# Scaling two finished super-blocks by the last norm on POOL instead of DVE, in an fp32 streaming-encoder kernel

## The chip, the cores and the metric

One core of one Trainium2 chip runs the whole kernel. The metric is the device time in microseconds, the median of several runs.

## What is computed

One layer of a hybrid trunk over 2080 columns (2064 prompt frames with 16 learned ones in front, less the 16, plus 32 sampled ones), model width 1024, feed-forward width 2816, all in float32. A mixer (convolution, gated recurrence, pooled branch) gives x1; then comes the feed-forward part and a last RMS norm, which alone matters here:

```
x = x + (silu(g) * u) @ w_down          # [g | u] = RMSNorm(x) @ w_gu
y = x * rsqrt(mean(x*x, axis=-1) + 1e-6) * final_g
```

## The kernel before

All data lie transposed: the model width on 128 partitions times 8 tiles, frames along the free axis. The mixer runs over five blocks of 416 columns. Then the feed-forward part runs over three **super-blocks** `s` = 0, 1, 2 of 696, 692 and 692 columns (two halves of 348 or 346), and this part is the place of the change.

**Order of a super-block.** `STEPS` is gu0, gu1, gu2, dn0, gu3, gu4, dn1 and so on: gate/up passes over eleven pairs of feed-forward tiles, and down passes over five groups of them. A gate/up pass makes seven products (one level of Strassen's scheme), each from one weight slot of 128x1024. Every fp32 product is made of three matmuls on a high and a low part, so each slot is split first: SP loads it into `wraw`, ACT writes the high part (L878), DVE the low part (L1720), and TensorE waits for the low part (L684). The slots go round a ring of three, and a slot is refilled as soon as TensorE has left it. TensorE's matmuls are all at L704.

**DVE's other work** in a pass, in program order: it adds products from PSUM (L1625), multiplies gate and up (L1672), forms differences (L1674, L1676), writes low parts of the result (L1678, L1691, L1696, L1698), and reads the seventh product (L1682, L1685). In a down pass it adds products into `xacc` (L1711), the fp32 accumulator of the super-block, 8 tiles of 128 x 692 or 696.

**The last norm of super-block s** is spread over the first passes of super-block s+1. In pass 0 ACT squares and DVE sums; TensorE sums over partitions; in pass 1 ACT takes the root (L1122) and DVE the reciprocal (L1612), which leaves `nrstd`, one 128 x 696 tile. Then `finish` (L1617) scales the tiles of `xacc` in the order `NORM_ORDER`, one DVE operation a tile, at the places that `FINISH` names: four in pass 1, four at the start of pass 2. Each adds one to the semaphore `y_done`.

**Who waits for y_done.** POOL, whose loop (L670 to L679) stores each tile to the output as it is done (L678), then waits for the first four stores to have landed, loads four tiles of the next super-block's x1 into the same `xacc` (L604), waits for the last four stores and loads the other four. The first additions of down pass 0 (L1711) wait for these loads. And ACT, which in pass 2 waits for all eight (L1172) before it writes `hcomb` (L1174), since that part of `hcomb` lies over `nrstd`; ACT's later splits are queued behind this wait. After the last super-block DVE makes its eight `finish` operations with nothing beside them.

Of the kernel before, what the change touches and what calls it, by code (L numbers as in the profile page):

```python
# [8 lines left out]
KT = D // P  # L9
SEQ, META, DEC = 2048, 16, 32  # L10
NB = 5
# [22 lines left out]
TH = (348, 346, 346)  # L34
# [17 lines left out]
G1, CW0, CB, BR, BI, LAM, PSC, G2, GF = 0, 1, 5, 6, 7, 8, 9, 10, 11  # L52
# [124 lines left out]
RAWS = {(s, i): n for n, (s, _, i) in enumerate(STORED)}  # L177
NSIDE = 4 * NB + 4
NORM_ORDER = (0, 4, 1, 5, 2, 6, 3, 7)
FINISH = {(1, 1): (0,), (1, 2): (1,), (1, 3): (2,), (1, 4): (3,), (2, 0): (4, 5), (2, 1): (6, 7)}  # L180
CORDER = (0, 5, 1, 4, 2, 3, 6)
CFROM = {0: 11, 5: 11, 1: 11, 4: 11, 2: 3, 3: 7, 6: 11}
DIFFS = ("T1", "T3", "T2", "T4")
# [89 lines left out]
def build(nc, dx, dwm, dws, dcst, dfix, dst0, graw, draw, dy, dst, fused, sgu, sdn, x1s, ys):  # L273
# [4 lines left out]
    MUL, ADD, SUB = ALU.mult, ALU.add, ALU.subtract  # L278
    base = -(-nc.sbuf_base // 64) * 64
    ctx = ExitStack()  # L280
    with ctx:
        def sem(name):
            return ctx.enter_context(nc.semaphore(name))

        def at(offset, name, shape, dt=f32):
            return nc.alloc_sbuf_tensor_at(name, shape, dt, offset=base + offset)
# [5 lines left out]
        cst = at(37376, "cst", [P, NCST, KT])  # L292
# [27 lines left out]
        xacc = at(m0, "xacc", [P, KT, 2 * HW])  # L320
        hcomb = at(m0 + 22272, "hcomb", [P, 3, 2, 7, HW], f32r)
        nsq, ntot = at(m0 + 61248, "nsq", [P, 2, 2 * HW]), at(m0 + 66816, "ntot", [P, 2 * HW])
        nrstd, nsum = at(m0 + 69600, "nrstd", [P, 2 * HW]), at(m0 + 72384, "nsum", [P, 2, 2 * HW], f32r)
# [10 lines left out]
        n_sq, n_sum, n_hi, n_lo, n_rstd = sem("n_sq"), sem("n_sum"), sem("n_hi"), sem("n_lo"), sem("n_rstd")  # L334
# [22 lines left out]
            "xb_t", "xb_hist", "xb_saved", "wsum", "wfix", "d_done", "d_hi", "d_lo"))  # L357
        merged, m_hi, m_lo = sem("merged"), sem("m_hi"), sem("m_lo")
        h_hi, h_lo = sem("h_hi"), sem("h_lo")
        y_done = sem("y_done")  # L360
        block = ctx.enter_context(nc.Block())

        def bank(name):
# [167 lines left out]
        def _(pool):  # L531
# [68 lines left out]
            def load_acc(s):  # L600
                for n, m in enumerate(NORM_ORDER):
                    if s and n % 4 == 0:
                        pool.wait_ge(y_stored[n // 4], 16 * 4 * s)
                    pool.dma_start(xacc[:, m, 0:2 * TH[s]], x1s[m, :, TO[s]:TO[s] + 2 * TH[s]]).then_inc(x1_in[n // 4], 16)  # L604

            def quarter(s, kh, h, first, landed):

                cols = slice(TO[s] + h * TH[s], TO[s] + h * TH[s] + TH[s])
                pool.dma_start(work[:, first:first + 4, 0:TH[s]],
                               ys[4 * kh:4 * kh + 4, :, cols].rearrange("k p c -> p k c")).then_inc(landed, 16)  # L610

            def plain_quarters(s):
                if s:
                    pool.wait_ge(a_lo, 7 * s)
                quarter(s, 0, 0, 11, y_in[0])
                pool.wait_ge(a_lo, 7 * s + 1)
                quarter(s, 1, 0, 11, y_in[0])
                pool.wait_ge(a_lo, 7 * s + 2)
                quarter(s, 1, 1, 11, y_in[0])

            def mixed_quarters(s):
                quarter(s, 0, 0, 3, y_in[1])
                quarter(s, 0, 1, 7, y_in[2])

            def last_quarter(s):
                pool.wait_ge(a_lo, 7 * s + 6)
                quarter(s, 1, 0, 7, y_in[2])
# [42 lines left out]
            for s in range(NT - 1):  # L670
                pool.wait_ge(y_kept, 16 * KT * NB)
                plain_quarters(s + 1)
                pool.wait_ge(h_lo, 4 * PAIRS * (s + 1))
                mixed_quarters(s + 1)
                last_quarter(s + 1)
                for n, m in enumerate(NORM_ORDER):
                    pool.wait_ge(y_done, 8 * s + n + 1)
                    pool.dma_start(dy[m, :, TO[s]:TO[s] + 2 * TH[s]], xacc[:, m, 0:2 * TH[s]]).then_inc(y_stored[n // 4], 16)  # L678
                load_acc(s + 1)  # L679
# [648 lines left out]
        def _(dve):  # L1328
# [5 lines left out]
            def square_sum(kind, b, m):  # L1334
                n = sq_index(kind, b, m)
                width = W if (kind, b) == ("n1", 0) else LW
                dve.wait_ge(sq_done, n + 1)
                if m == 0:
                    V.tensor_copy(tot[:, 0:width], sq[:, n % 2, 0:width]).then_inc(sq_summed, 1)
                else:  # L1340
                    dve.wait_ge(sq_summed, n)
                    V.tensor_tensor(tot[:, 0:width], tot[:, 0:width], sq[:, n % 2, 0:width], ADD).then_inc(sq_summed, 1)

            def sum_rest(kind, b):
                dve.wait_ge(sum_hi, sum_index(kind, b) + 1)
                V.tensor_tensor(sums[:, 1, :], tot[:, 0:LW], sums[:, 0, :].bitcast(f32), SUB).then_inc(sum_lo, 1)

            def invert(name, q):
                b = name[1]
                width = LW if q else W  # L1350
                dve.wait_ge(*(clear(name) if name == ("n2", NB - 1, 0) else drain(name)))
                V.reciprocal(rstd[q][:, 0:width], rstd[q][:, 0:width]).then_inc(rstd_done[q], 1)
                dve.wait_ge(rstd_done[q], b if q == 1 else b + 1)
# [26 lines left out]
            def make_y(b, m):  # L1380
                if m == 0:
                    dve.wait_ge(x1_kept, 16 * KT * (b + 1))
                V.scalar_tensor_tensor(main[:, m, :], main[:, m, :], cst[:, G2, m:m + 1], rstd[2][:, 0:LW], MUL, MUL).then_inc(y_made, 1)
# [182 lines left out]
            def operand_lo(s, c):  # L1566
                w, q = TH[s], CORDER.index(c)
                dve.wait_ge(a_hi, 7 * s + q + 1)
                V.tensor_tensor(ycomb[:, c, 1, :, 0:w], work[:, CFROM[c]:CFROM[c] + 4, 0:w],
                                ycomb[:, c, 0, :, 0:w].bitcast(f32), SUB).then_inc(a_lo, 1)  # L1570
# [24 lines left out]
            def norm_sum(s, i):  # L1595
                n, w = KT * s + i, 2 * TH[s]
                dve.wait_ge(n_sq, n + 1)
                if i == 0:
                    V.tensor_copy(ntot[:, 0:w], nsq[:, n % 2, 0:w]).then_inc(n_sum, 1)
                else:  # L1600
                    dve.wait_ge(n_sum, n)
                    V.tensor_tensor(ntot[:, 0:w], ntot[:, 0:w], nsq[:, n % 2, 0:w], ADD).then_inc(n_sum, 1)

            def norm_rest(s):
                w = 2 * TH[s]
                dve.wait_ge(n_hi, s + 1)
                V.tensor_tensor(nsum[:, 1, 0:w], ntot[:, 0:w], nsum[:, 0, 0:w].bitcast(f32), SUB).then_inc(n_lo, 1)

            def norm_invert(s):
                w = 2 * TH[s]  # L1610
                dve.wait_ge(*clear(("n3", s, 0)))
                V.reciprocal(nrstd[:, 0:w], nrstd[:, 0:w]).then_inc(n_rstd, 1)  # L1612

            def finish(s, i):
                w, m = 2 * TH[s], NORM_ORDER[i]
                dve.wait_ge(n_rstd, s + 1)
                V.scalar_tensor_tensor(xacc[:, m, 0:w], xacc[:, m, 0:w], cst[:, GF, m:m + 1], nrstd[:, 0:w], MUL, MUL).then_inc(y_done, 1)  # L1617
# [9 lines left out]
            def beside(s, p, k):  # L1627


                if (p, k) == (0, 0):  # L1630
                    operand_lo(s, 6)
                if p == 0 and k < 4:
                    for i in (2 * k, 2 * k + 1):
                        if s:
                            norm_sum(s - 1, i)
                        else:
                            square_sum("n2", NB - 1, i)
                elif (p, k) == (0, 4):
                    if s:
                        norm_rest(s - 1)  # L1640
                    else:
                        sum_rest("n2", NB - 1)
                elif (p, k) == (1, 0):
                    if s:
                        norm_invert(s - 1)
                    else:
                        invert(("n2", NB - 1, 0), 2)
                for i in FINISH.get((p, k), ()):
                    if s:
                        finish(s - 1, i)  # L1650
                    else:
                        make_y(NB - 1, i)

            def gate_up(s, p):
                n, w, z = s * PAIRS + p, TH[s], p % 3
# [298 lines left out]
```

## Time and profile before

| | us |
|---|---|
| median of 3 runs (2748.52 to 2753.92) | 2750.82 |
| profiled execution | 2748.8 |
| its span, first to last instruction | 2747.0 |
| TensorE (PE) busy | 2681.8 (98%) |
| VectorE (DVE) busy | 2059.0 (75%) |
| ScalarE (ACT) busy | 1358.9 (49%) |
| GpSimd (POOL) busy | 192.9 (7%) |

An engine's busy time is the sum of its instructions. A timeline row gives start, duration, engine, line, operation, tiles and shapes, how many instructions it merges, and in brackets the idle time before it and what ended it. A row of who waited for whom gives the total, the number of times and the longest.

### The profile page before, as it was taken

How to read it: one execution, taken by the hardware profiler on the slowest of the kernel's cores; microseconds unless marked ns; L12 is line 12 of the kernel's file. 1: busy time of each engine (PE TensorE's matmuls, PEld its weight loads, DVE VectorE, ACT ScalarE, POOL GpSimd, SP SyncE). 2: the span in 40 equal slices, each digit the busy share in tenths (PEclk: the TensorE clock that was granted, in tenths of full speed). 3: DMA queues.
4: the chain of work that ended last, by engine and by line, in shares of the span. 5: the costliest groups of instructions: out<-in, count | busy, mean ns of one | idle time of the engine just before them, and what ended most of it. 6: DMA issues, size and time to landing. Idle time of an engine off the chain costs nothing.

```text
span 2747.0 us, 39191 instructions
## 1 busy us (share of the span) xinstructions
PE 2681.8 (98%) x15404; PEld 2651.8 (97%) x15404; DVE 2059.0 (75%) x2723; ACT 1358.9 (49%) x1822; POOL 192.9 (7%) x369
## 2 busy tenths in 40 slices
PE   8999999999999999999999999999999999999995
PEld 7999999999999999999999999999999999999995
DVE  7868787788878877887777676688667688676666
ACT  6743484358436743663454344454434345344442
POOL 2000101020101011101100000001000000000000
PEclk9999999999999999999999999999999999999998
DMA  7453567546765767566564444456444454644443
GB/s 241 132 186 115 192 222 268 190 162 228 253 202 172 235 220 233 172 231 210 199 205 133 144 138 138 141 160 235 130 144 136 139 160 163 207 137 139 131 131 99
DMA packets 149254, 486.10 MB, mean 177 GB/s; under 512 B 16464, under 2 KB 34000, under 8 KB 149072
## 3 DMA queue, kind: packets, MB, share of 16 engines
q1 hardware_dynamic: 106224, 345.21, 38.5%
q0 software_dynamic: 32336, 121.92, 12.9%
q10 hardware_dynamic: 10512, 16.46, 2.0%
q8 instruction: 124, 2.03, 0.3%
q14 instruction: 58, 0.48, 0.1%
HBM read 419.01 MB, written 64.51 MB: 176 GB/s over the span
## 4 chain that ended last, share of the span: by engine, by line
PE 76%; DVE 12%; issue 5%; ACT 4%; DMA 2%; SPq 0%; DVEq 0%; ACTq 0%
PE ps L704 75%; DVE wring L1720 2%; ACT wring L878 1%; DVE work L1672 1%; DMA work<-ys 1%; ACT work L1147 1%; DVE work L1625 1%; DVE ga L1841 1%; DVE xacc L1711 1%; DVE work L1674 1%; DVE tmp L1839 1%; DMA wraw<-dwm 1%; DMA wraw<-draw 1%; DVE hcomb L1678 1%; DVE nrstd L1612 0%
## 5 line engine op out<-in xcount | busy, mean ns | idle before, releaser
L704 PE MATMUL ps<-ycomb,wring 128*128 128x346 f32 (+1 forms) x5544 | 884.7, 321 | 9.6 <-DVE wring L1720 5.7
L704 PEld LDWEIGHTS ps<-ycomb,wring 128*128 128x128 f32 x5544 | 880.8, 188 | 11.6 <-DVE wring L1720 6.9
L1720 DVE TENSOR_TENSOR wring<-wraw,wring 128x1024 fp32r<-128x1024 f32 x529 | 644.9, 1220 | 261.8 <-ACT wring L878 260.1
L878 ACT ACTIVATE wring<-wraw 128x1024 fp32r<-128x1024 f32 x529 | 557.1, 1054 | 443.9 <-PE ps L704 422.6
L704 PE MATMUL ps<-xhi,wring 128*128 128x416 f32 (+1 forms) x1728 | 478.3, 353 | 11.8 <-DVE wring L1720 8.9
L704 PE MATMUL ps<-yhi,wring 128*128 128x416 f32 x1568 | 429.5, 351 | 0.4 <-DVE ylo L1364 0.4
L704 PEld LDWEIGHTS ps<-xhi,wring 128*128 128x128 f32 x1728 | 326.4, 189 | 16.6 <-issue 12.4
L704 PE MATMUL ps<-hcomb,wring 128*128 128x346 f32 (+1 forms) x2016 | 325.6, 322 | 4.7 <-DVE xacc L1711 4.7
L704 PEld LDWEIGHTS ps<-hcomb,wring 128*128 128x128 f32 x2016 | 320.6, 188 | 8.0 <-DVE xacc L1711 8.0
L704 PE MATMUL ps<-xlo,wring 128*128 128x416 f32 (+1 forms) x864 | 305.2, 353 | 0.0
L704 PEld LDWEIGHTS ps<-yhi,wring 128*128 128x128 f32 x1568 | 294.3, 188 | 2.8 <-issue 0.7
L704 PE MATMUL ps<-ylo,wring 128*128 128x416 f32 x784 | 275.1, 351 | 0.0
L1711 DVE TENSOR_TENSOR xacc<-ps,xacc 128x692 f32<-128x692 f32 (+1 forms) x210 | 179.0, 872 | 39.0 <-PE ps L704 39.0
L1106 ACT ACTIVATE work<-ps 128x692 f32<-128x692 f32 (+1 forms) x99 | 74.1, 748 | 193.9 <-PE ps L704 193.7
L704 PEld LDWEIGHTS ps<-xlo,wring 128*128 128x128 f32 x864 | 163.1, 189 | 2.8
L704 PE MATMUL ps<-xhi,wextra 128*128 128x416 f32 (+1 forms) x576 | 162.1, 352 | 0.0
L704 PEld LDWEIGHTS ps<-ylo,wring 128*128 128x128 f32 x784 | 147.1, 188 | 1.7
L1625 DVE TENSOR_TENSOR work<-ps,work 128x692 f32<-128x692 f32 (+1 forms) x99 | 86.8, 877 | 71.0 <-PE ps L704 71.0
L704 PE MATMUL ps<-yhi,wextra 128*128 128x416 f32 x480 | 134.7, 352 | 0.0
L704 PE MATMUL ps<-hcomb,wlast 128*128 128x346 f32 (+1 forms) x756 | 122.7, 322 | 7.8 <-DVE wlast L1720 5.0
L704 PEld LDWEIGHTS ps<-hcomb,wlast 128*128 128x128 f32 x756 | 119.9, 188 | 10.4 <-issue 10.4
L704 PEld LDWEIGHTS ps<-xhi,wextra 128*128 128x128 f32 x576 | 108.2, 188 | 1.4
(236 smaller groups left out, 2922.8 us busy)
## 6 DMA issues: line engine op xcount, KB each, us to landing
wraw<-dwm SPq DMA_DIRECT2D x247, 512.0 KB, 3.9
wraw<-sgu SPq DMA_DIRECT2D x132, 512.0 KB, 3.3
wraw<-graw SPq DMA_DIRECT2D x99, 512.0 KB, 3.5
wraw<-sdn SPq DMA_DIRECT2D x48, 512.0 KB, 3.6
pbuf<-graw POOLq DMA_DIRECT2D x22, 1024.0 KB, 7.5
sgu<-pbuf POOLq DMA_DIRECT2D x22, 1024.0 KB, 6.1
wraw<-fused SPq DMA_DIRECT2D x40, 512.0 KB, 3.3
wraw<-draw SPq DMA_DIRECT2D x36, 512.0 KB, 3.7
```

What stands on the lines that cost most here:

```text
L704: mm = nc.tensor.matmul(out, wt[:, c * P:(c + 1) * P], x, start=(first and q == 0), stop=(last and q == 2), skip_group_check=chain)
L878: A(ring(n)[:, 0, 0:c], wraw[:, n % RAW, 0:c], ACT.Copy, scale=cst[:, PSC, name[2]:name[2] + 1] if name[0] == "w" else 1.0).then_inc(w_hi, 1)
L1106: A(work[:, first:first + 8:7, 0:TH[s]], both(name, TH[s]), ACT.Copy).then_inc(cleared[BANK[name] // 2], 1)
L1147: A(work[:, 0:3, 0:w], work[:, 0:3, 0:w], ACT.Silu).then_inc(silu3, 1)
L1625: V.tensor_tensor(c, both(name, TH[s]), c, ADD).then_inc(cleared[BANK[name] // 2], 1)
L1672: V.tensor_tensor(work[:, 7:10, 0:w], work[:, 7:10, 0:w], work[:, 0:3, 0:w], MUL).then_inc(h_mult, 1)
L1674: V.tensor_tensor(work[:, 3:5, 0:w], work[:, 8:10, 0:w], work[:, 7:9, 0:w], SUB).then_inc(h_diff, 1)
L1678: V.tensor_tensor(hl[:, 0:2, :], work[:, 7:10:2, 0:w], hh[:, 0:2, :].bitcast(f32), SUB).then_inc(h_lo, 1)
L1711: V.tensor_tensor(out, both(name, w), out, ADD).then_inc(cleared[BANK[name] // 2], 1)
L1720: V.tensor_tensor(ring(n)[:, 1, 0:c], wraw[:, n % RAW, 0:c], ring(n)[:, 0, 0:c].bitcast(f32), SUB).then_inc(w_lo, 1)
L1839: V.tensor_tensor(tmp[:, 3 + 4 * (m % 2), 0:LW], bank(name)[:, 0:LW], gb[:, m, 0:LW], MUL).then_inc(drained[BANK[name]], 1)
L1841: V.tensor_tensor(ga[:, m, :], ga[:, m, :], tmp[:, 3 + 4 * (m % 2), 0:LW], ADD).then_inc(merged, 1)
```

## The change

For the first two super-blocks `finish` is taken out of DVE's program, and POOL does the scaling, ahead of its loop of stores: it waits for the reciprocal (`n_rstd`), and for each tile it multiplies `xacc` by `nrstd` in place, waits for that by a new semaphore `y_scaled`, and multiplies by the tile's column of `final_g` in place, which adds one to `y_done`. The third super-block stays with DVE. `FINISH` is renamed `MAKE_Y`, since on DVE it now places the operations `make_y` of the norm before the feed-forward part alone, as it did before for s = 0.

```diff
-        y_done = sem("y_done")
+        y_done, y_scaled = sem("y_done"), sem("y_scaled")
...
                 last_quarter(s + 1)
+                pool.wait_ge(n_rstd, s + 1)
+                for n, m in enumerate(NORM_ORDER):
+                    out = xacc[:, m, 0:2 * TH[s]]
+                    nc.gpsimd.tensor_tensor(out, out, nrstd[:, 0:2 * TH[s]], MUL).then_inc(y_scaled, 1)
+                    pool.wait_ge(y_scaled, KT * s + n + 1)
+                    nc.gpsimd.tensor_scalar(out, out, cst[:, GF, m:m + 1], None, MUL).then_inc(y_done, 1)
                 for n, m in enumerate(NORM_ORDER):
                     pool.wait_ge(y_done, 8 * s + n + 1)
                     pool.dma_start(dy[m, :, TO[s]:TO[s] + 2 * TH[s]], xacc[:, m, 0:2 * TH[s]]).then_inc(y_stored[n // 4], 16)
...
-                for i in FINISH.get((p, k), ()):
-                    if s:
-                        finish(s - 1, i)
-                    else:
-                        make_y(NB - 1, i)
+                for i in () if s else MAKE_Y.get((p, k), ()):
+                    make_y(NB - 1, i)
```

## Rows read from the trace of the kernel before

**Rows 1.** The page's busy times, share of the span and instruction counts of each engine.

```profile
PE 2681.8 (98%) x15404; PEld 2651.8 (97%) x15404; DVE 2059.0 (75%) x2723; ACT 1358.9 (49%) x1822; POOL 192.9 (7%) x369
```

**Rows 2.** Whom TensorE waited for, first passage, 1855 to 1912 us.

```profile
PE ps L704 <- DVE wring L1720: 1.1, 1, 1.1
PE ps L704 <- DVE xacc L1711: 0.4, 1, 0.4
```

**Rows 3.** TensorE's timeline of the second passage: start, duration, count, in brackets the wait.

```profile
2311.92 42.14 PE L704 MATMUL ps<-ycomb,wring 128*128 128x346 f32 x264 [1.06 <-DVE wring L1720]
...
2362.99 19.31 PE L704 MATMUL ps<-hcomb,wring 128*128 128x346 f32 x120 [1.32 <-DVE xacc L1711]
```

**Rows 4.** Instructions of line 1617: count, duration in ns (min/median/max), first and last start.

```profile
L1617 DVE SCALAR_TENSOR_TENSOR xacc<-xacc,cst,nrstd x24: 928/933/939, 1860.4 to 2743.0; 128x692 f32<-128x692 f32 x16, 128x696 f32<-128x696 f32 x8
```

**Rows 5.** DVE's timeline at the start of the first passage.

```profile
1854.94 4.50 DVE L1612 RECIPROCAL nrstd<-nrstd 128x696 f32<-128x696 f32 x1 [0.42 <-ACT nrstd L1122]
```

**Rows 6.** POOL's timeline, early in the kernel: small elementwise operations.

```profile
13.23 1.23 POOL L541 TENSOR_TENSOR lac<-lac 128x8 f32<-128x8 f32 x1 [12.80 <-DVE lac L1753]
14.55 1.06 POOL L542 TENSOR_TENSOR lac<-lac 128x8 f32<-128x8 f32 x1
...
26.96 0.20 POOL L548 TENSOR_TENSOR lac<-lac 128x8 f32<-128x8 f32 x1
...
39.29 0.19 POOL L565 COPY tbuf<-state 128x3 f32<-128x3 f32 x1 [8.14 <-DVE gb L1409]
```

**Rows 7.** DVE's timeline at the same places.

```profile
13.18 2.37 DVE L1720 TENSOR_TENSOR wring<-wraw,wring 128x1024 fp32r<-128x1024 f32 x2
...
26.83 2.85 DVE L1352 RECIPROCAL rstd_n<-rstd_n 128x432 f32<-128x432 f32 x1 [1.26 <-ACT rstd_n L926]
...
39.26 0.61 DVE L1391 TENSOR_TENSOR tbuf<-ps,rstd_n 128x432 f32<-128x432 f32 x1
```

**Rows 8.** TensorE's timeline of the first passage.

```profile
1860.58 42.14 PE L704 MATMUL ps<-ycomb,wring 128*128 128x346 f32 x264 [1.08 <-DVE wring L1720]
```

**Rows 9.** Line 1720 alone, by stretch: length, DVE busy (instructions), clock, DMA share, GB/s.

```profile
1859.30:1873.30 14.00, 6.03 (x5) 1.00 0.78 261
```

**Rows 10.** DVE's timeline inside the first passage.

```profile
1874.40 1.24 DVE L1672 TENSOR_TENSOR work<-work 128x1038 f32<-128x1038 f32 x1 [1.21 <-ACT work L1147]
1875.67 0.88 DVE L1674 TENSOR_TENSOR work<-work 128x692 f32<-128x692 f32 x1
1876.59 0.52 DVE L1676 TENSOR_TENSOR work<-work 128x346 f32<-128x346 f32 x1
1877.02 1.22 DVE L1720 TENSOR_TENSOR wring<-wraw,wring 128x1024 fp32r<-128x1024 f32 x1
1878.16 0.87 DVE L1678 TENSOR_TENSOR hcomb<-work,hcomb 128x692 fp32r<-128x692 f32 x1
1878.95 0.51 DVE L1682 TENSOR_TENSOR work<-ps,work 128x346 f32<-128x346 f32 x1
...
1879.93 1.23 DVE L1691 TENSOR_TENSOR hcomb<-work,hcomb 128x1038 fp32r<-128x1038 f32 x1
1881.08 1.22 DVE L1720 TENSOR_TENSOR wring<-wraw,wring 128x1024 fp32r<-128x1024 f32 x1
...
1884.78 1.22 DVE L1720 TENSOR_TENSOR wring<-wraw,wring 128x1024 fp32r<-128x1024 f32 x1
...
1909.79 1.65 DVE L1711 TENSOR_TENSOR xacc<-ps,xacc 128x692 f32<-128x692 f32 x2
```

**Rows 11.** ACT's timeline: its first operation behind the wait for y_done.

```profile
1902.44 0.79 ACT L1174 ACTIVATE hcomb<-work 128x692 fp32r<-128x692 f32 x1
```

**Rows 12.** POOL's timeline: the last store and the second four loads, first passage.

```profile
1888.00 0.54 POOL L678 DMA_DIRECT2D dy<-xacc  x1 [0.31 <-DVE xacc L1617]
...
1893.48 2.12 POOL L604 DMA_DIRECT2D xacc<-x1s  x4 [2.81 <-DMA dy<-xacc]
```

**Rows 13.** DMA issues around 1895.1: queue, count, KB, us from issue to landing.

```profile
xacc<-x1s POOLq DMA_DIRECT2D x2, 346.0 KB, 9.6
```

More of the change, by code:

```diff
@@ L179 @@
 NORM_ORDER = (0, 4, 1, 5, 2, 6, 3, 7)
-FINISH = {(1, 1): (0,), (1, 2): (1,), (1, 3): (2,), (1, 4): (3,), (2, 0): (4, 5), (2, 1): (6, 7)}
+MAKE_Y = {(1, 1): (0,), (1, 2): (1,), (1, 3): (2,), (1, 4): (3,), (2, 0): (4, 5), (2, 1): (6, 7)}
 CORDER = (0, 5, 1, 4, 2, 3, 6)
```

## The prediction

> **What bounds the kernel now.** I read the page first, then who waited for whom on TensorE, then the timelines of DVE, POOL and ACT in the two stretches that the change touches. The reader should see in the page that PE is busy for 98% of the span and POOL for 7% [rows 1]. So the engine that is relieved (DVE, 75%) bounds nothing as a whole, and what counts is the time that TensorE loses to it in those two stretches, the passages, which begin with the reciprocals of super-blocks 0 and 1. In the first TensorE waits 1.1 us for a split weight slot and 0.4 us for an addition into xacc [rows 2], in the second 1.1 and 1.3 us [rows 3]: 3.9 us in all. That is the most that the change could win, 0.14% of 2748.8. The two waits for a slot come from the 4.5 us reciprocal in front of the split [rows 5], which stays. The wait for an addition in the first passage comes at 1909.8 [rows 10], 22 us after the last scaling, which ended when the last store went out at 1888.0 [rows 12]; I take it that a scaling does not reach so far, and keep the 3.9 us as the bound.
>
> **What is removed.** 16 of the 24 scalings of line 1617, 0.93 us each [rows 4], 14.9 us of DVE time. They lie between DVE operations that TensorE doesn't wait for now [rows 2, 3]. Worth: 0.
>
> **What is added on POOL.** 8 tiles by 2 operations in each passage, and a wait between the two of a tile. POOL has nothing else to do then; it is waiting for y_done. The trace has no POOL operation of this width. An 8-element multiply takes 0.20 us there [rows 6], so the fixed part is small. For the wide part the nearest rows are DVE's: 0.93 us for the fused scaling [rows 4] from below, and 4.5 us for the reciprocal of the same tile [rows 5] from above. I take 1.7 us for the multiply of two tiles and 1.0 us for the multiply by a column; an ordinary multiply is nearer to the scaling than to a reciprocal. A pair is 2.7 us, eight pairs are 21.6 us.
>
> The Trainium skill, "GPSIMD Engine Reference", section "Performance versus the Vector engine", has 4497 ns for a two-input fp32 operation on 2048 elements, and calls one-input operations roughly line-rate under "When to use GPSIMD". In proportion that is an estimate of 1.5 us for the first of a pair; with it the sum below would be about 2 us smaller. No row here shows it.
>
> **The term that decides: the two engines get in each other's way.** POOL's first two 8-element operations took 1.23 and 1.06 us and ended at 14.46 and 15.61 [rows 6]. DVE's two splits beside them, which read two SBUF tiles, ran from 13.18 to 15.55, so one ended at about 14.4 and one at 15.55 [rows 7]. Each POOL operation ended just behind one DVE operation: it could not run beside it, and it got its turn between the two. Beside a reciprocal, which reads one tile, POOL took 0.20 us, and beside an operation that reads PSUM and one SBUF tile 0.19 us [rows 6, 7]. So a POOL operation that reads and a DVE operation that reads two SBUF tiles exclude each other, and they alternate. In those rows POOL pays, because its operations are tiny. Whether DVE pays when a long POOL operation is first, no row shows; the bounds are nothing and the whole POOL operation. I take the whole, since the same exclusion seen from the other side gives it.
>
> The Trainium skill states this for both sides, in "SBUF — State Buffer", section "Who interferes with whom": a DVE instruction with two SBUF inputs contends with a GpSimd instruction that reads SBUF, and whichever starts first keeps the shared interface for its whole length. The trace agrees for the side that it shows, with the 1.23 us above. By that rule this change is bad; without it the sum would be 0 to 7 us, as in the rivals.
>
> Now the first passage. The scaling begins at 1859.4. TensorE runs 264 matmuls in 42.14 us, 0.160 us each [rows 8]; a slot of 24 lasts 3.83 us. Counted from 1860.58 slots begin at 1879.7, 1883.6 and 1887.4. The split for them is now done at 1878.2, 1882.2 and 1885.9 [rows 10], so the slack is 1.5, 1.4 and 1.5 us.
>
> Up to 1873.3 DVE has five splits, 6.03 us [rows 9], with idle time between. Alternating with these POOL gets six of its operations done (6.03 + 8.1 = 14.1 us) and is in its seventh, until 1875.0. DVE falls behind from there. All its operations in [rows 10], and L1685 behind L1682, read two SBUF tiles, but for L1682 and L1711 (PSUM).
> - Split of slot 1: the seventh POOL operation holds L1672 by 0.6 us; three more (1.0, 1.7, 1.0) stand ahead of L1674, L1676 and the split. Late by 4.3: 1882.5 against 1879.7. TensorE stalls 2.8 us.
> - Split of slot 2: four more, ahead of L1678, L1685, L1691 and the split (1.7, 0.5 since half of it runs beside L1682, 1.7, 1.0). Late by 9.2: 1891.4 against 1883.6 + 2.8. Stall 5.0 us.
> - Split of slot 3: the last two POOL operations (2.7), less two scalings that are gone (1.7). Late by 10.2: 1896.1 against 1887.4 + 7.8. Stall 0.9 us.
>
> The sum is 8.7 us a passage. POOL ends at about 1894.4, 35 us after it began, not at 1887.7 as DVE does now. The second passage has the same order of work, so 17.4 us in all. With 0.9 us for each POOL operation the same walk gives about 1.1, 3.7 and 0, 9.6 us in all.
>
> **What is queued behind POOL.** The eight stores now follow the last scaling, where before seven were out. Now the last store is issued at 1888.00 [rows 12], 0.3 us after the last scaling, the second loads from 1893.48, and the last, issued near 1895.1, lands 9.6 us later, at 1904.7 [rows 13]: 17.0 us behind the last scaling. In the changed kernel seven further issues of 0.54 us stand between, 3.8, and more data are under way at once; I take 21.5 us, so 1915.9. DVE's first addition needs it at 1909.79 [rows 10], but by then TensorE and DVE are 8.7 us late: 1918.5. Cost 0, cover 2.6 us. ACT's wait for all eight ends at 1894.4 against 1902.44 [rows 11]; cost 0, cover 8 us and more. Behind that wait stand ACT's splits, which TensorE would miss at once. Loading the first quarter of the next operands, behind these loads on POOL, is wanted some 300 us later: 0.
>
> **Sum.** Profiled execution 2748.8 + 17.4 = 2766.2. The median of the runs is 2.0 above the profiled one: 2768.
>
> **Rivals.**
> 1. POOL's reads don't hold DVE, or only briefly, and POOL is done by 1889, 30 us after it began (a pair of 2.7 and 16 waits of 0.5). For it: no row shows DVE held, and its splits fill only 6.03 of 14 us [rows 9]. Against it: the alternation in [rows 6, 7]. Then the loads land by 1910.5 and nothing is late. This is the case that is not slower: 2751, decided by POOL's total of 30 us or less and a DVE that isn't held.
> 2. DVE isn't held, but POOL is held behind it, ending at 1892.5 or somewhat later. The loads land at 1914 against 1910.7, 3.3 us a passage, 6.6 in all: 2757. The wait of additions for x1 takes the place of nothing.
> 3. A POOL pair costs much more, 4 us and up (towards the reciprocal's price). With 50 us in all the loads land at 1859.4 + 50 + 21.5 = 1931, 20 us behind 1910.7, and ACT is held from 1902.4 too: 40 us in all, 2791.
> 4. The relief of DVE shortens the waits of [rows 2, 3] and nothing else changes: 2747.
>
> **How the numbers follow.** Forecast 0.51, rival 1 0.27, rival 2 0.12, rival 3 0.07, rival 4 0.03. What a measurement of this kernel can tell from no change is about 0.2%, 5.5 us. Slower by more: forecast, rival 3 and most of rival 2, 0.67. Within: rival 1 and the rest, 0.30. Faster: 0.03, as all of 3.9 us would not reach the bound by itself. The range goes from 2749.5, under rival 1, to 2787, between the forecast with POOL operations half as long again and rival 3. The forecast's own range is 2760 to 2780.
>
> **What would show it.** Slot splits (L1720) in the passages that start late with POOL named or with no releaser, or DVE operations of two SBUF tiles that take 2 to 3 us instead of 1.2; TensorE waiting about 8 us in each passage for L1720; POOL operations of 1 to 3 us that end just behind DVE's. Rival 1: TensorE's waits as in [rows 2, 3], and the scaling over by 30 us. Rival 2: waits for L1711 alone, with xacc loads as the releaser. Rival 3: POOL operations above 3 us with DVE idle. I am wrong in the sum if DVE takes its turn first each time, or if the slack of a slot is larger than the 1.5 us read above.

## The result: 0.85% slower

The changed kernel takes 2774.7 us (median of 6 runs, 2770.7 to 2776.0) against 2750.1 us for the kernel before on the same chips: a ratio of 1.0085, 95% interval 1.0072 to 1.0098. That is 24.6 us more. The direction, the range and the place were as forecast; the amount was 17.4 us in the forecast, and it is made up in part of other terms than I wrote.

The page of the profiled execution of the changed kernel, span and busy times (to set against [rows 1], which has a span of 2747.0):

```profile
span 2771.8 us, 39207 instructions
PE 2693.1 (97%) x15404; PEld 2661.6 (96%) x15404; DVE 2064.7 (74%) x2707; ACT 1358.9 (49%) x1822; POOL 270.6 (10%) x401
```

DVE has 16 instructions less, 14.9 us of work, and yet it is busy for 5.7 us more than before. POOL's additional 77.6 us are the scaling. (The added code moves the lines: splits are L1723 here, additions into xacc L1714, matmuls L710.)

TensorE's timeline of the first passage (start, duration, count, in brackets the wait before), which answers to [rows 8] and [rows 2]:

```profile
1860.14 19.30 PE L710 MATMUL ps<-ycomb,wring 128*128 128x346 f32 x120 [1.08 <-DVE wring L1723]
1879.76 4.07 PE L710 MATMUL ps<-ycomb,wring 128*128 128x346 f32 x24 [0.32 <-DVE wring L1723]
1886.88 20.71 PE L710 MATMUL ps<-ycomb,wring 128*128 128x346 f32 x120 [3.04 <-DVE wring L1723]
1907.42 7.77 PE L710 MATMUL ps<-hcomb,wring 128*128 128x346 f32 x48
1918.19 3.83 PE L710 MATMUL ps<-hcomb,wring 128*128 128x346 f32 x12 [2.99 <-DVE xacc L1714]
1922.90 19.50 PE L710 MATMUL ps<-hcomb,wring 128*128 128x346 f32 x108 [0.89 <-DVE xacc L1714]
```

The unbroken run of 264 matmuls of [rows 8] is cut by two late splits (0.32 and 3.04 us), and two late additions follow (2.99 and 0.89 us, where it was 0.4). But that is not all: the 120 matmuls behind 3.04 us of waiting take 20.71 us instead of 19.30, and the 12 behind 2.99 us take 3.83 us, 0.32 each and not 0.16. The same stretches with the granted clock (length, PE busy and instructions, clock, DMA share, GB/s) show why:

```profile
1886.85:1890.20 3.35, 3.33 (x12) 0.52 0.47 157
1917.60:1927.80 10.20, 8.73 (x29) 0.51 0.65 238
1927.80:1937.80 10.00, 10.00 (x66) 1.00 0.43 154
```

TensorE was granted half its speed (1.2 instead of 2.4 GHz) for 3.4 us around the first long wait and for 10.2 us around the second. The first half-speed stretch costs 1.4 us, by the 120 matmuls (20.71 against 19.30); in the second 29 matmuls took 8.73 us, where 29 at 0.16 us are 4.6, so 4.1 us.

The bill of the first passage, in us: late splits 3.4, half clock behind them 1.4, late additions 3.5 (3.9 less the 0.4 of before), half clock behind them 4.1. Sum 12.4. Measured from the first matmul shown to the start of the next gate/up products it is 82.1 us against 69.3 before, 12.8 more; the 0.4 us between the two figures I have not taken apart. The second passage repeats it: 0.30 and 3.02 for splits, 3.23 and 0.98 for additions (where it was 1.3), half clock for 3.4 and 10.2 us, 12.2 us in all. The spans differ by 24.8.

### The profile page after: what moved, and what is told of

Read it like the earlier page. It is cut to its first block, busy times and chain, and to the rows that moved or that the text cites. A ratio compares the mean times of both kernels' runs of the same rounds, so it can differ in the third digit from the quotient of the medians.

```text
span 2771.8 us, 39207 instructions
## 1 busy us (share of the span) xinstructions
PE 2693.1 (97%) x15404; PEld 2661.6 (96%) x15404; DVE 2064.7 (74%) x2707; ACT 1358.9 (49%) x1822; POOL 270.6 (10%) x401
## 3 DMA queue, kind: packets, MB, share of 16 engines
q8 instruction: 124, 2.03, 0.3%
## 4 chain that ended last, share of the span: by engine, by line
PE 74%; DVE 11%; issue 5%; ACT 4%; DMA 3%; POOL 3%; SPq 0%; DVEq 0%; ACTq 0%
PE ps L710 74%; POOL xacc L681 2%; ACT wring L884 1%; POOL xacc L679 1%; DVE wring L1723 1%; DMA work<-ys 1%; DVE work L1675 1%; DMA xacc<-x1s 1%; DVE ga L1844 1%; ACT work L1153 1%; DVE tmp L1842 1%; DVE xacc L1714 1%; DMA dy<-xacc 1%; DMA wraw<-dwm 1%; DVE work L1631 1%
## 5 line engine op out<-in xcount | busy, mean ns | idle before, releaser
L710 PE MATMUL ps<-ycomb,wring 128*128 128x346 f32 (+1 forms) x5544 | 888.6, 322 | 17.4 <-DVE wring L1723 13.9
L710 PEld LDWEIGHTS ps<-ycomb,wring 128*128 128x128 f32 x5544 | 883.7, 189 | 20.5 <-DVE wring L1723 16.2
L1723 DVE TENSOR_TENSOR wring<-wraw,wring 128x1024 fp32r<-128x1024 f32 x529 | 655.4, 1240 | 263.3 <-ACT wring L884 261.6
L710 PE MATMUL ps<-xhi,wring 128*128 128x416 f32 (+1 forms) x1728 | 478.3, 353 | 12.0 <-DVE wring L1723 9.0
L710 PE MATMUL ps<-yhi,wring 128*128 128x416 f32 x1568 | 429.5, 351 | 0.4 <-DVE ylo L1370 0.4
L710 PE MATMUL ps<-hcomb,wring 128*128 128x346 f32 (+1 forms) x2016 | 333.5, 327 | 11.1 <-DVE xacc L1714 11.1
L710 PEld LDWEIGHTS ps<-hcomb,wring 128*128 128x128 f32 x2016 | 327.7, 192 | 15.3 <-DVE xacc L1714 15.3
L710 PEld LDWEIGHTS ps<-xhi,wring 128*128 128x128 f32 x1728 | 326.2, 189 | 16.7 <-issue 12.6
L710 PE MATMUL ps<-xlo,wring 128*128 128x416 f32 (+1 forms) x864 | 305.2, 353 | 0.0
L710 PEld LDWEIGHTS ps<-yhi,wring 128*128 128x128 f32 x1568 | 294.3, 188 | 2.8 <-issue 0.7
L710 PE MATMUL ps<-ylo,wring 128*128 128x416 f32 x784 | 275.1, 351 | 0.0
L1714 DVE TENSOR_TENSOR xacc<-ps,xacc 128x692 f32<-128x692 f32 (+1 forms) x210 | 179.5, 872 | 53.9 <-PE ps L710 44.7
L710 PEld LDWEIGHTS ps<-xlo,wring 128*128 128x128 f32 x864 | 163.1, 189 | 2.8
L710 PE MATMUL ps<-xhi,wextra 128*128 128x416 f32 (+1 forms) x576 | 162.1, 352 | 0.0
L710 PEld LDWEIGHTS ps<-ylo,wring 128*128 128x128 f32 x784 | 147.0, 188 | 1.8
L710 PE MATMUL ps<-yhi,wextra 128*128 128x416 f32 x480 | 134.7, 352 | 0.0
L710 PE MATMUL ps<-hcomb,wlast 128*128 128x346 f32 (+1 forms) x756 | 122.8, 322 | 7.2 <-DVE wlast L1723 4.6
L710 PEld LDWEIGHTS ps<-hcomb,wlast 128*128 128x128 f32 x756 | 120.0, 188 | 9.8 <-issue 9.8
L710 PEld LDWEIGHTS ps<-xhi,wextra 128*128 128x128 f32 x576 | 108.2, 188 | 1.4
```

Source lines behind the costliest of these rows:

```text
L710: mm = nc.tensor.matmul(out, wt[:, c * P:(c + 1) * P], x, start=(first and q == 0), stop=(last and q == 2), skip_group_check=chain)
L1714: V.tensor_tensor(out, both(name, w), out, ADD).then_inc(cleared[BANK[name] // 2], 1)
L1723: V.tensor_tensor(ring(n)[:, 1, 0:c], wraw[:, n % RAW, 0:c], ring(n)[:, 0, 0:c].bitcast(f32), SUB).then_inc(w_lo, 1)
```

## Where the waits come from

POOL's timeline of the first passage, in part:

```profile
1859.09 2.54 POOL L679 TENSOR_TENSOR xacc<-xacc,nrstd 128x696 f32<-128x696 f32 x1 [49.11 <-DVE nrstd L1618]
1861.74 3.94 POOL L681 TENSOR_SCALAR xacc<-xacc,cst 128x696 f32<-128x696 f32 x1
1865.65 1.69 POOL L679 TENSOR_TENSOR xacc<-xacc,nrstd 128x696 f32<-128x696 f32 x1
1867.45 2.89 POOL L681 TENSOR_SCALAR xacc<-xacc,cst 128x696 f32<-128x696 f32 x1
1870.31 1.69 POOL L679 TENSOR_TENSOR xacc<-xacc,nrstd 128x696 f32<-128x696 f32 x1
1872.10 2.03 POOL L681 TENSOR_SCALAR xacc<-xacc,cst 128x696 f32<-128x696 f32 x1
1874.09 2.67 POOL L679 TENSOR_TENSOR xacc<-xacc,nrstd 128x696 f32<-128x696 f32 x1
...
1898.49 4.36 POOL L684 DMA_DIRECT2D dy<-xacc  x8
1906.54 2.14 POOL L604 DMA_DIRECT2D xacc<-x1s  x4 [3.69 <-DMA dy<-xacc]
1912.01 2.12 POOL L604 DMA_DIRECT2D xacc<-x1s  x4 [3.33 <-DMA dy<-xacc]
```

DVE's timeline beside it, in part, which answers to [rows 10]:

```profile
1865.99 2.44 DVE L1723 TENSOR_TENSOR wring<-wraw,wring 128x1024 fp32r<-128x1024 f32 x1 [2.14 <-ACT wring L884]
1868.36 0.86 DVE L1631 TENSOR_TENSOR work<-ps,work 128x692 f32<-128x692 f32 x1
1869.22 1.22 DVE L1723 TENSOR_TENSOR wring<-wraw,wring 128x1024 fp32r<-128x1024 f32 x1
...
1875.24 2.25 DVE L1677 TENSOR_TENSOR work<-work 128x692 f32<-128x692 f32 x1
1877.52 1.05 DVE L1679 TENSOR_TENSOR work<-work 128x346 f32<-128x346 f32 x1
1878.49 1.21 DVE L1723 TENSOR_TENSOR wring<-wraw,wring 128x1024 fp32r<-128x1024 f32 x1
1879.63 2.37 DVE L1681 TENSOR_TENSOR hcomb<-work,hcomb 128x692 fp32r<-128x692 f32 x1
...
1884.15 2.67 DVE L1723 TENSOR_TENSOR wring<-wraw,wring 128x1024 fp32r<-128x1024 f32 x1
```

Here DVE is the one that pays, which no row of before showed. A split that starts at 1865.99, while POOL multiplies two tiles, is recorded with 2.44 us and not 1.22: it is held until POOL's two-tile multiply, which began at 1865.65, is done at 1867.3. L1677 takes 2.25 instead of 0.88, L1681 2.37 instead of 0.87. The split at 1884.15 ends at 1886.8, and TensorE restarts at 1886.88. The multiply by a column is another matter: the split at 1869.22 runs beside it, in its plain 1.22 us. DVE isn't the only one that pays: POOL's column multiply at 1861.74 took 3.94 us and not 2.03, beside two splits.

The rest is a chain: the last scaling ends at 1898.5, all eight stores are issued behind it, the loads wait for the stores. Whom DVE waited for, 1855 to 1930 us (total, times, longest):

```profile
DVE xacc L1714 <- DMA xacc<-x1s: 6.4, 2, 3.8
```

The last load lands at 1921.9, 23.4 us behind the last scaling; TensorE would have had use for the addition from 1915.2.

## The experiments

My theory after the result: (a) POOL's two-tile multiply holds DVE's two-tile operations, and this makes splits late; (b) the scaling ends late and its stores and loads stand behind it, and this makes additions late; (c) each long wait costs half clock besides. The rivals: held DVE operations explain everything; every POOL operation costs its share wherever it is; DVE's relief itself changes something. The pieces are taken one by one.

**One of POOL's two operations at a time**

```diff
-                    nc.gpsimd.tensor_tensor(out, out, nrstd[:, 0:2 * TH[s]], MUL).then_inc(y_scaled, 1)
-                    pool.wait_ge(y_scaled, KT * s + n + 1)
-                    nc.gpsimd.tensor_scalar(out, out, cst[:, GF, m:m + 1], None, MUL).then_inc(y_done, 1)
+                    nc.gpsimd.tensor_tensor(out, out, nrstd[:, 0:2 * TH[s]], MUL).then_inc(y_done, 1)
```

> The changed kernel with only the first of POOL's two operations a tile (the multiply by the norm); the multiply by the final weights is left out for the first two super-blocks. Theory (DVE operations of two SBUF tiles are held while a POOL operation reads, and the scaling that ends late makes the x1 loads late): POOL done after about 19 us a passage, so no wait for x1 loads; DVE held by about 1.2 us for each of 8 operations, DVE busy near 2063 us, but spread where there is slack, so TensorE loses 0 to 1.5 us a passage: 2750 to 2753. Rival (each POOL operation costs TensorE its share, half of the 24.6 us): 2762.

Measured: 2755.9 us, ratio 1.0022 (1.0012 to 1.0031). The second kernel keeps the other operation:

```diff
+                    nc.gpsimd.tensor_scalar(out, out, cst[:, GF, m:m + 1], None, MUL).then_inc(y_done, 1)
```

> The changed kernel with only the second of POOL's two operations a tile (the multiply by a column, one SBUF tile read); the multiply by the norm is left out for the first two super-blocks. Theory (this operation holds DVE only while it reads, about 0.6 of its 2.0 us): DVE busy near 2050 us, POOL done after about 22 us, time 2750. Rival (the lock holds for the whole instruction): DVE busy near 2063 us or above, splits late as with the other half, 2752 to 2762.

Measured: 2749.9 us, ratio 1.0001 (0.9992 to 1.0010).

**No scaling at all for the first two super-blocks**

```diff
-                for n, m in enumerate(NORM_ORDER):
-                    out = xacc[:, m, 0:2 * TH[s]]
...
+                for n in range(KT):
+                    nc.gpsimd.memset(rstd2[:, 0:1], 0.0).then_inc(y_done, 1)
+                    pool.wait_ge(y_done, KT * s + n + 1)
```

> The changed kernel with no scaling of the first two super-blocks by any engine (it is left out); POOL waits for the reciprocal, makes eight memsets of one column in its place and stores. Both theories: DVE is relieved of 14.9 us and nobody is held up; if the relief is worth nothing the time is 2750, with TensorE's waits for L1720 at the start of each passage as before. A theory by which the relief itself is worth something (DVE bounds these stretches): 2746 or less.

Measured: 2749.5 us, ratio 1.0002 (0.9992 to 1.0011). So the relief of 14.9 us of DVE time is worth nothing that can be measured in the time.

The busy times of the three kernels, in this order (two-tile multiply only, column multiply only, none), from their pages:

```profile
PE 2683.6 (97%) x15404; PEld 2653.6 (96%) x15404; DVE 2058.1 (75%) x2707; ACT 1358.5 (49%) x1822; POOL 231.1 (8%) x385
```

```profile
PE 2686.9 (98%) x15404; PEld 2658.1 (97%) x15404; DVE 2048.9 (74%) x2707; ACT 1358.8 (49%) x1822; POOL 229.2 (8%) x385
```

```profile
PE 2683.8 (98%) x15404; PEld 2653.9 (96%) x15404; DVE 2046.9 (74%) x2707; ACT 1359.1 (49%) x1822; POOL 194.8 (7%) x385
```

All three have the same DVE instructions, 2707. What DVE's busy time has above that of the last is time in which it was held: 11.2 us for sixteen two-tile multiplies, 0.7 us each, and 2.0 us for sixteen column multiplies, 0.13 us each. In the changed kernel it is 17.8 us. Such a difference of two profiles is good to about a microsecond (the kernel before and the one with 26 memsets below have the same DVE instructions and differ by 1.3 us), but DVE's timeline agrees. With the column multiply alone two DVE operations of the first passage are longer than usual, by 0.56 and 0.55 us, and no other:

```profile
1874.12 1.78 DVE L1721 TENSOR_TENSOR wring<-wraw,wring 128x1024 fp32r<-128x1024 f32 x1 [0.27 <-ACT wring L882]
1880.13 1.43 DVE L1675 TENSOR_TENSOR work<-work 128x692 f32<-128x692 f32 x1
```

With the two-tile multiply alone the operations of the first passage are longer by 5.9 us together. POOL's eight operations took 19.1 us of the first passage with the two-tile multiply and 18.0 with the column multiply:

```profile
1860.96 19.06 POOL L679 TENSOR_TENSOR xacc<-xacc,nrstd 128x696 f32<-128x696 f32 x8 [47.49 <-DVE nrstd L1616]
```

```profile
1864.01 18.00 POOL L679 TENSOR_SCALAR xacc<-xacc,cst 128x696 f32<-128x696 f32 x8 [50.52 <-DVE nrstd L1616]
```

So holding comes nearly all from the multiply that reads two tiles, and part (a) stands: POOL is done equally early in both kernels, and only the one with this multiply has a late split. The expectation for the column multiply held (DVE held for about 0.6 of its 2.0 us, DVE busy near 2050, time 2750). My number for the first kernel was too low: a loss of 5.6 us and not 0 to 3. Its TensorE timeline of the first passage:

```profile
1882.51 23.35 PE L708 MATMUL ps<-ycomb,wring 128*128 128x346 f32 x144 [1.19 <-DVE wring L1721]
1905.69 7.77 PE L708 MATMUL ps<-hcomb,wring 128*128 128x346 f32 x48
1914.86 10.43 PE L708 MATMUL ps<-hcomb,wring 128*128 128x346 f32 x64 [1.39 <-DVE xacc L1712]
```

A split is late by 1.19 us even so, and the first addition waits 1.39 us instead of 0.38 (on that wait see the last experiment). The "share" rival (12 us) is out: eight two-tile multiplies alone cost 2 to 3 us a passage.

**Stores along with the scaling.** POOL issues the store of a tile behind the scaling of the next one:

```diff
+                    if n:
+                        i = NORM_ORDER[n - 1]
+                        pool.wait_ge(y_done, KT * s + n)
+                        pool.dma_start(dy[i, :, TO[s]:TO[s] + 2 * TH[s]], xacc[:, i, 0:2 * TH[s]]).then_inc(y_stored[(n - 1) // 4], 16)
```

> The changed kernel, but each tile's store is issued by POOL behind the next tile's scaling, not all eight behind the last. Theory (about half of the loss is the late x1 loads and the half clock behind that wait): POOL's last scaling ends some 4 us later, but the loads are issued 4 to 5 us earlier; the waits for slot splits and the half clock behind them stay, about 5 to 6 us a passage, the waits for additions fall to 0 to 1 us: 2761 to 2764. Rival (the loss is all held DVE operations): no change, 2774.

Measured: 2761.7 us, ratio 1.0047 (1.0032 to 1.0062): 13 us of the 24.6 are back, as expected. TensorE's timeline of the first passage:

```profile
1879.25 4.08 PE L712 MATMUL ps<-ycomb,wring 128*128 128x346 f32 x24 [0.63 <-DVE wring L1725]
1887.21 21.82 PE L712 MATMUL ps<-ycomb,wring 128*128 128x346 f32 x120 [3.88 <-DVE wring L1725]
1908.87 7.77 PE L712 MATMUL ps<-hcomb,wring 128*128 128x346 f32 x48
1916.96 19.30 PE L712 MATMUL ps<-hcomb,wring 128*128 128x346 f32 x120 [0.32 <-DVE xacc L1716]
```

The splits are late as in the changed kernel, and by 0.3 and 0.8 us more (0.63 and 3.88), with half clock behind them (21.82 us for 120 matmuls), and the waits for additions with their half clock are gone. All operations of the scaling are still there, so the other half of the loss was the order of stores and loads and not the held DVE.

**Late stores with nothing held.** DVE scales as in the kernel before. POOL waits for all eight tiles, then spends time on memsets of an unused tile, which read nothing:

```diff
+                pool.wait_ge(y_done, KT * (s + 1))
+                for n in range(26):
+                    nc.gpsimd.memset(rstd2[:, 0:LW], 0.0).then_inc(y_scaled, 1)
+                    pool.wait_ge(y_scaled, 26 * s + n + 1)
                 for n, m in enumerate(NORM_ORDER):
                     pool.wait_ge(y_done, 8 * s + n + 1)
```

> The kernel before, DVE scaling as it did, but POOL waits for all eight tiles and then runs 26 small memsets of an unused tile one behind the other (about 0.45 us each, they read nothing) before it stores. Theory: no split is late; stores and x1 loads are late as in the changed kernel and TensorE, which isn't held up before, meets them earlier: a wait of about 12 us a passage for the additions of L1711 and half clock for some 10 us behind it, 16 us a passage, 2782. Rival (the loads have slack enough, or the loss comes from held DVE operations): 2750.

Measured: 2771.9 us, ratio 1.0083 (1.0068 to 1.0098), which is 10 us less than I expected. With 12 memsets:

> As the run with 26 memsets, but with 12 (6.0 us). Theory (slack of the loads 4.3 us, and a wait of that length lets TensorE's clock fall only if it is long): a wait of 1.5 to 2.5 us a passage, and the cost beyond the wait shows whether the clock falls: 2754 without, 2760 to 2763 with half clock for about 10 us behind each wait. Rival (the loads aren't the cause): 2750.

Measured: 2764.0 us, ratio 1.0054 (1.0039 to 1.0069). And with none, so that only the order is changed:

> The kernel before, DVE scaling as it did, but POOL waits for all eight tiles before it stores the first. The eight stores then stand behind the last scaling as in the changed kernel, 3.8 us of further issues ahead of the loads. Theory (the x1 loads have about 4.3 us of slack, from the 13.0 us of memsets that made 9.0 us of waiting): the loads come about 4 us later and are just in time, 0 to 0.5 us a passage, 2750 to 2751. Rival (the order of the stores alone is a good part of the late loads): a wait of over 2 us for L1711 in each passage and half clock behind it, 2755 or more.

Measured: 2751.6 us, ratio 1.0006 (0.9997 to 1.0015). TensorE in the first passage, for 26 memsets:

```profile
1860.77 42.14 PE L708 MATMUL ps<-ycomb,wring 128*128 128x346 f32 x264 [1.08 <-DVE wring L1724]
1919.56 21.92 PE L708 MATMUL ps<-hcomb,wring 128*128 128x346 f32 x120 [9.04 <-DVE xacc L1715]
```

for 12:

```profile
1916.12 2.16 PE L708 MATMUL ps<-hcomb,wring 128*128 128x346 f32 x12 [2.29 <-DVE xacc L1715]
1922.68 18.68 PE L708 MATMUL ps<-hcomb,wring 128*128 128x346 f32 x108 [4.40 <-DVE xacc L1715]
```

and for none:

```profile
1912.09 2.18 PE L705 MATMUL ps<-hcomb,wring 128*128 128x346 f32 x12 [0.31 <-DVE xacc L1712]
1915.61 17.41 PE L705 MATMUL ps<-hcomb,wring 128*128 128x346 f32 x108 [1.34 <-DVE xacc L1712]
```

No split is late in any of them, and the loss is there: part (b) stands by itself. The slack of the loads is what I had wrong, twice. Storing all eight behind the last scaling already uses it up (1.34 us of waiting; the 0.31 in front of it is what TensorE waits there when nothing is late), and 6.0 us more make 6.7 us of waiting in the first passage and 4.7 in the second, not 2. For part (c): with 26 memsets TensorE waits 9.0 and 9.6 us in the two passages, with 12 it waits 6.7 and 4.7. Less the 0.4 and 1.3 us of the kernel before that is 17.0 and 9.7 us of waiting, and the losses are 21.6 and 14.2 us by the medians, so that 4.6 us of each are not waiting. A stretch of half clock is there in both; for 26 memsets it was 1915.0 to 1925.3 in the first passage:

```profile
1915.00:1925.30 10.30, 5.74 (x20) 5.53 (x21) 3.96 (x5) 0.00 (x0) 1.17 (x2) 0.50 0.73 281
```

but nearly half of it falls into the wait itself, where a slow clock costs nothing. It costs 2.6 us in the first passage (21.92 against 19.30) and 1.8 in the second. In the changed kernel the wait is shorter, and most of the stretch falls on matmuls: 4.1 us. No run separates (c) from the waits. It rests on the clock and the matmul durations of the traces.

**Half of the tiles on POOL.** The diff shows the two places that matter; the waits for the scaled tiles are changed to match.

```diff
+                for n, m in enumerate(NORM_ORDER[:4]):
...
+                    elif i >= 4:
+                        finish(s - 1, i)
```

> The changed kernel with half of the tiles: POOL scales the first four tiles in two operations each, DVE the last four at its old places in pass 2. Theory (the second of the late splits is hit by the POOL operations behind the eighth, and the loads by POOL's total): POOL done after 20 us, first late split by 0.3 us, second in time, loads in time; 2750 to 2752. Rival (every tile on POOL costs TensorE its share of the loss): half of 24.6, 2762.

Measured: 2755.2 us, ratio 1.0018 (1.0009 to 1.0028). POOL was done after 20.3 us and the splits were late by 0.32 us, as expected, but TensorE waited 1.55 us for the first addition and the median is 3 us above what I expected. The profile is of the fastest of the ten executions (2751.7 us), and shows less than the median's loss. A quarter of the loss for half of the tiles: the cost isn't proportional, and it does not start at zero. That it grows once the ninth and later POOL operations meet the tightest splits and the loads fits the changed kernel's timeline, but no other run tries it.

**A kernel that should beat both.** The 1.1 us waits at the start of each passage come from the reciprocal. Cut in two halves with the split between:

```diff
-                V.reciprocal(nrstd[:, 0:w], nrstd[:, 0:w]).then_inc(n_rstd, 1)
+                V.reciprocal(nrstd[:, v * w:v * w + w], nrstd[:, v * w:v * w + w]).then_inc(n_rstd, 1)
...
+                if s and (p, k) == (1, 1):
+                    norm_invert(s - 1, 1)
```

> The kernel before with the reciprocal of the last norm (4.5 us on DVE) cut in two halves of 2.2 us, the split that TensorE waits for between them. Theory (the 1.1 us waits at the start of the two passages come from the reciprocal in front of the split, and nothing else in the passage is tight): the waits are gone, 2.1 us, 2748; the median will hardly tell it from 2750, the profile will. Rival (the second half makes the next split or addition late): the wait moves behind it, 2750 or 2751.

Measured: 2750.5 us, ratio 0.9998 (0.9989 to 1.0007). In its profile:

```profile
1866.52 38.31 PE L704 MATMUL ps<-ycomb,wring 128*128 128x346 f32 x240 [0.23 <-DVE wring L1722]
1904.66 7.77 PE L704 MATMUL ps<-hcomb,wring 128*128 128x346 f32 x48
1913.48 19.31 PE L704 MATMUL ps<-hcomb,wring 128*128 128x346 f32 x120 [1.04 <-DVE xacc L1713]
```

The 1.08 us became 0.23 on the next slot, and TensorE waited 1.04 us for the first addition instead of 0.38. Of 3.9 us that could be had in both passages 1 us was had. No run beat the kernel before.

What ends these short waits for the first addition isn't the x1 load; DVE doesn't wait for that here. Followed back from TensorE's wait at 1910.7, the profile of the kernel before goes through the DVE and ACT operations of pass 2 to the load of a weight slot, which took 7.1 us (the median of these loads in the page is 3.7), and from there to the split that left the slot's `wraw` free, behind the scalings (start, duration, what):

```profile
1886.00 1.71 DVE xacc L1617 x2
1888.50 1.14 DVE wring L1720
1889.65 7.11 DMA wraw<-draw
```

The load of the same slot stands behind the 1.32 us of the kernel before in the second passage (8.1 us), the 1.39 us of the two-tile multiply alone (8.9), the 1.55 us of half of the tiles (7.6) and the 1.04 us here (7.8). With no scaling at all the chain leads to TensorE itself, and the wait is 0.32 us in both passages. So leaving the scaling off DVE is worth about 1 us after all, in the second passage, which the profile shows and the median doesn't. Whether the slot's load comes late because it starts late or because stores and x1 loads are under way beside it, no run separates.

## Why the prediction was right, point by point

- **What bounds the kernel, and that DVE's relief is worth 0:** right for the time. Without any scaling it is 2749.5 us. But "I take it that a scaling does not reach so far" was wrong: the scalings stand in the chain of the wait for the first addition, as shown above, and without them the 1.3 us of the second passage are 0.3. The bound of 3.9 us holds.
- **The price on POOL.** The two-tile multiply was taken at 1.7 us and is 1.69 where nothing holds it. The column multiply was taken at 1.0 us and is 2.03 at the least, 2.25 on average by itself. This term was off by a factor of two: it was priced by DVE's row [rows 4], and POOL's own 8-element row says nothing of a wide one. In all the scaling took 39.4 us, not 35, and part of it was waiting for DVE. The Trainium skill, "GPSIMD Engine Reference", section "When to use GPSIMD", says that one-input operations run roughly at line rate; at 696 elements the measured 2.03 us are more than the 1.69 us of the two-input one, so here the measurement decides against it.
- **That POOL holds DVE:** right for the two-tile multiply (0.7 us each on average), wrong for the column multiply (0.13 us on average, about 0.55 us where it held one at all). This is the step that was mis-sized: "I take the whole" for both. The Trainium skill, "SBUF — State Buffer", section "Who interferes with whom", calls the shared port pair an exclusive lock, and says of DVE's two-port modes that whoever issues first gets it for the whole instruction. The trace agrees for two tiles (a split held until 1867.3, the end of POOL's 1.69 us) and not for the column multiply, beside which a split ran in 1.22 us and which held others by 0.55 us. The alternation wasn't strict either: the column multiply at 1861.74 took 3.94 us.
- **The late splits:** the right splits in the right order, but TensorE stalled 0.3, 3.0 and 0 us for them instead of 2.8, 5.0 and 0.9. That is 3.4 us instead of 8.7 a passage.
- **What is queued behind POOL:** wrong. "Cost 0, cover 2.6 us" rested on an end of the scaling at 1894.4 and on TensorE being 8.7 us late by then. POOL ended 4.1 us later (1898.5), the loads took 23.4 instead of 21.5 us, and TensorE was less late. The cost was 3.5 us in the first passage and 2.9 in the second. So the late loads, which are the core of rival 2, came beside the forecast and not instead of it; I had treated the two as exclusive.
- **The clock** is missing from the sum altogether, 5.5 us in the first passage, over two fifths of the loss. I priced a wait of 3 us at 3 us.
- **ACT's wait for y_done:** right, cost 0; nothing in ACT's waits names it.

Two errors of opposite sign, splits too dear by 5.3 us and loads and clock left out, 9.0 us in the first passage, brought the sum to 70% of the truth. The direction and the places of the late splits came from the mechanism; that the amount was so near was in part luck.

## What to carry to other kernels

Before work is moved to an idle engine, ask who waits for its result and what is queued behind it there. The operations were off the critical path on DVE because they were short and their stores went out one by one; on POOL, at four times the price a tile (2.0 + 1.7 us and waits against 0.93), the loads behind them were on it. Look for the tightest slack (here 1.5 us for a slot split), not for the busy share of the engine that is relieved, and try the relief alone first: in the time it was worth nothing. A wait of some 3 us on TensorE must be priced with the half clock that may follow it. And follow a short wait back through its chain before giving it a cause: the engine that is named last need not be the late one.

## What the runs showed of the hardware

- A DVE operation that is held by POOL is recorded with a longer duration (2.44 instead of 1.22 us), not as idle time. Only a comparison with the usual duration of the same form shows it, and no view of waits names POOL.
- POOL's multiply of a 128x696 tile by a column (2.03 us at least) is slower than its multiply of two tiles (1.69 us), but holds DVE far less (2.0 us for sixteen, against 11.2 us).
- After waits of 3.0 us TensorE ran at half clock for 3.4 us in one place and for 10.2 us in another. In the second place two waits, 2.99 and 0.89 us, lay close together; what makes the stretch longer wasn't tried. After waits of 1.19 and 1.39 us (two-tile multiply alone) the granted clock stayed at 1.00, and after one of 2.29 us (12 memsets) the next 12 matmuls still ran at full clock, in 2.16 us.
